# Output projections as sums of rounded products, and an experts' loop without its marker products

## Chip, cores and metric

The kernel runs on one core of a Trainium2 chip. The metric is the device time of one execution in microseconds: the median of the runs shown. TensorE (PE) does the matrix products, PEld its weight loads, VectorE (DVE) and ScalarE (ACT) the elementwise work, GpSimd (POOL) and SyncE (SP) start transfers; each engine works through its own instruction list in order, and semaphores tie the lists together.

## The reference

Two blocks work on 256 tokens of 1024 columns (the first also on 256 context tokens); all in float32.

```python
# first block, layer 0
y = concat([fourier_mix(a), neighborhood_attention(q, k, v, ...)]) @ w_out      # 512 tokens, 1024 x 1024
# both layers
for e in range(N_EXPERTS):                                                      # 16 experts, top 2 of them per token
    hid = silu(tok @ w1[e]) * (tok @ w3[e])
    out = out + gate[:, e:e + 1] * (hid @ w2[e])
# second block
y_a = (attention * silu(g_a)) @ w_proj_a                                        # 512 -> 1024
y_b = o_b @ w_proj_b                                                            # 1024 -> 1024
merged = sigmoid(zgate_a) * y_a + sigmoid(zgate_b) * y_b
h_res = h_res + merged @ w_out                                                  # 1024 -> 1024
```

## The kernel before

Activations lie transposed, 128 columns of the model on the partitions and the tokens along the free axis: `hT` is the residual stream, `XT` the working copy, `arena` a region that each stage lays out anew. All weights come through a ring of three slots of 2 MB (`ring`, `SLOTS`, `BLK`): SP waits until a slot is free (`w_free`), starts the load of the next block (L511), and readers wait for `w_full`. The order of the blocks is fixed (`B_MIX`, `B_MIXO`, `B_MOE0`, ...).

Most projections are already sums of rounded products. A weight part of 128 x 1024 elements is rounded by ACT to float32r (`..._hi`), DVE subtracts that from the weight and writes the rest back into the ring (`..._lo`), the activations are split in the same way, and TensorE adds three float32r products per step (`three_terms`, L622, and `quarter`, L721): high times high, low times high, high times low. Four places still use plain float32 products through `chain` (L576): the first block's output projection (L964 to L972, blocks `B_MIXO`, 8 tiles of 8 products with 512 tokens), the retention output projection (L1055), and in the second block `B_PA` (L1267, 8 tiles of 4 products with 256 tokens), `B_PB` (L1274, 8 tiles of 8) and `B_WO` (L1285, 8 tiles of 8). In the trace one float32 product in `chain` is two records.

The first of these follows the neighborhood attention loop (L923 to L962), which is a software pipeline over 24 pairs in `NA_PAIRS`: the first 12 have 512 keys, the last 12 have 256. In step i TensorE makes the scores of pair i (L930), turns the probabilities of pair i-2 (L945) and multiplies pair i-3 by the values (L959); DVE finds the row maximum (L1978), scales (L1984, L1986) and copies a result out (L1993); ACT copies (L1491) and exponentiates (L1499).

The experts' loop (`routed`) handles one expert per turn, and each layer has 16 turns. A turn has three blocks of four quarters: w1 (512 columns per product), w3 (256 columns) and w2 (512 columns), 24 products of `quarter` or `three_terms` for w1, 48 for w3, 24 for w2. `w_hi` and `w_lo` hold four quarters; ACT may round quarter q of the next block only when TensorE is done with quarter q of the present one, which it learns from `split_used`. [...] Where the last product of a quarter already raises another one (`f_u1`, `f_u3`, `f_d`), a marker product of two columns follows it and raises `split_used`:

```python
def used():
    nc.tensor.matmul(ps[0:32, 7, 0:2], tick[:, 0:32], tick[:, 0:2], start=True, stop=True).then_inc(split_used, 1)
```

That is four marker products (L588) in a turn: one behind w1, two in w3, one behind w2. `release` (L581) makes the same kind of product (L583) for the ring and stays.

The second block's attention (L1232 to L1263) is a similar pipeline over eight pairs in `AT_PAIRS`, with a DVE reduction (L2264), an ACT exponential (L1662), an ACT copy (L1657), turned probabilities (L1261) and the product with the values (L1252). Then come `B_PA`, `B_PB`, `B_WO` one after the other, each tile evicted by DVE (L2283; L2287 and L2288; L2291), and one transfer writes 1 MB to `out_d`.

## Time and profile before

| | us |
|---|---|
| time, median of 3 runs | 2014.21 (2013.33 to 2014.35) |
| the profiled execution's own time | 2023.89 |
| its span, first to last instruction | 2022.1 |
| TensorE busy in it | 1808.3 (89%) |
| VectorE / ScalarE busy | 1077.0 / 946.7 |
| mean granted TensorE clock | 0.942 of full speed |

The profile comes from one execution, so stages are compared inside it, and a difference in a stage is then set against the median. Busy TensorE time counts matmuls that overlap in the pipeline, so the distance between the starts of two matmuls says more than the duration of one.

### The profile page before, as it was taken

To read this page: it belongs to the slowest core of one execution; us is meant where nothing else is said; L and a number is where in the kernel's file an instruction comes from. 1 tells how busy PE (TensorE), PEld (TensorE's weight loads), DVE (VectorE), ACT (ScalarE), POOL (GpSimd) and SP (SyncE) were. 2 spreads that over 40 slices of the span, in tenths; PEclk is the share of its full clock that TensorE was granted. 3 is DMA by queue.
4 is the path that set the end of the run, shared out by engine and by line. 5 is a ranking of instruction groups with operands and counts; after the bars stand their busy time and mean duration, and the time that the engine had idled before them with its cause. 6 is when DMAs were issued, how large, how long until landed. Compare 5 with 4: busy or idle time off the path is not lost.

```text
span 2022.1 us, 27351 instructions
## 1 busy us (share of the span) xinstructions
PE 1808.3 (89%) x10936; PEld 1450.2 (72%) x10936; DVE 1077.0 (53%) x1423; ACT 946.7 (47%) x1234; POOL 60.9 (3%) x68
## 2 busy tenths in 40 slices
PE   5999998699999467999878789999947998999888
PEld 2786644588888437879757668888836988887677
DVE  3531623788888436243321278888835485534431
ACT  3323604588878315233320268788824472343320
POOL 0000000000000100000000010000000000100100
PEclk8999999799999778999989989999978999999899
DMA  8725014799999734224344369999951544263511
GB/s 333 149 108 208 1 42 173 284 379 389 384 377 380 293 122 160 84 88 162 126 166 167 146 262 385 371 392 383 368 223 67 187 167 149 69 203 145 146 43 63
DMA packets 52943, 421.68 MB, mean 209 GB/s; under 512 B 16996, under 2 KB 18148, under 8 KB 30576
## 3 DMA queue, kind: packets, MB, share of 16 engines
q1 hardware_dynamic: 26240, 364.55, 46.9%
q0 software_dynamic: 8592, 32.69, 5.2%
q10 hardware_dynamic: 18016, 23.07, 3.6%
q8 instruction: 73, 1.20, 0.2%
q14 instruction: 22, 0.18, 0.0%
HBM read 399.27 MB, written 21.02 MB: 208 GB/s over the span
## 4 chain that ended last, share of the span: by engine, by line
PE 84%; DVE 6%; DMA 3%; ACT 3%; issue 2%; POOL 0%; SPq 0%; DVEq 0%; ACTq 0%; POOLq 0%
PE ps L625 37%; PE ps L726 19%; PE ps L578 12%; PE ps L605 2%; PE ps L633 2%; PE ps L741 2%; PE ps L616 1%; PE ps L930 1%; PE ps L959 1%; PE ps L945 1%; DMA y_d<-arena 1%; PE ps L1120 1%; PE ps L748 1%; PE ps L588 1%; DMA hT<-h 1%
## 5 line engine op out<-in xcount | busy, mean ns | idle before, releaser
L1830 DVE TENSOR_TENSOR w_lo<-ring,w_hi 128x1024 fp32r<-128x1024 f32 x384 | 452.6, 1219 | 63.6 <-ACT w_hi L1366 63.6
L1366 ACT ACTIVATE w_hi<-ring 128x1024 fp32r<-128x1024 f32 x384 | 398.6, 1058 | 127.2 <-PE ps L588 43.2
L625 PE MATMUL ps<-XT_lo,arena_r 128*128 128x256 f32 (+1 forms) x1584 | 349.6, 297 | 8.9 <-DVE ring_r L2106 7.2
L625 PEld LDWEIGHTS ps<-XT_lo,arena_r 128*128 128x128 f32 x1584 | 260.9, 191 | 21.4 <-issue 7.9
L726 PE MATMUL ps<-w_hi,x_hi 128*128 128x256 f32 (+1 forms) x768 | 259.7, 338 | 4.8 <-issue 4.8
L726 PE MATMUL ps<-w_hi,x_lo 128*128 128x256 f32 (+1 forms) x768 | 246.3, 321 | 0.0
L726 PE MATMUL ps<-w_lo,x_hi 128*128 128x256 f32 (+1 forms) x768 | 246.2, 321 | 0.0
L625 PE MATMUL ps<-arena_r 128*128 128x512 f32 (+1 forms) x560 | 198.9, 355 | 15.6 <-DVE ring_r L2018 10.6
L2106 DVE TENSOR_TENSOR ring_r<-ring,arena_r 128x1024 fp32r<-128x1024 f32 x96 | 113.5, 1221 | 128.4 <-ACT arena_r L1588 128.3
L625 PE MATMUL ps<-XT_lo,ring_r 128*128 128x256 f32 x608 | 172.1, 283 | 0.0
L625 PE MATMUL ps<-w_hi,arena_r 128*128 128x512 f32 x512 | 161.1, 396 | 0.0
L726 PEld LDWEIGHTS ps<-w_hi,x_hi 128*128 128x128 f32 x768 | 146.5, 191 | 16.4 <-issue 5.6
L726 PEld LDWEIGHTS ps<-w_lo,x_hi 128*128 128x128 f32 x768 | 146.6, 191 | 11.2
L726 PEld LDWEIGHTS ps<-w_hi,x_lo 128*128 128x128 f32 x768 | 146.9, 191 | 9.7
L625 PEld LDWEIGHTS ps<-arena_r 128*128 128x128 f32 x560 | 107.5, 192 | 33.8 <-DVE ring_r L2018 10.7
L625 PE MATMUL ps<-arena_r,XT_lo 128*128 128x512 f32 (+1 forms) x352 | 126.1, 396 | 6.0 <-DVE XT_lo L2114 6.0
L578 PE MATMUL ps<-arena,ring 128*128 128x256 f32 x576 | 126.4, 381 | 1.3 <-DVE arena L2288 0.9
L625 PE MATMUL ps<-arena_r,ring_r 128*128 128x256 f32 (+1 forms) x368 | 125.2, 340 | 0.0
L2018 DVE TENSOR_TENSOR ring_r<-ring,arena_r 128x1024 fp32r<-128x1024 f32 x48 | 58.6, 1225 | 117.2 <-ACT arena_r L1526 117.1
L578 PEld LDWEIGHTS ps<-arena,ring 128*128 128x128 f32 x576 | 108.9, 190 | 16.0 <-DVE arena L2288 0.9
L625 PEld LDWEIGHTS ps<-XT_lo,ring_r 128*128 128x128 f32 x608 | 115.8, 190 | 0.0
L1306 ACT ACTIVATE XT<-hT 128x512 f32<-128x512 f32 (+1 forms) x48 | 20.5, 508 | 195.5 <-DVE hT L1881 66.7
(295 smaller groups left out, 2555.9 us busy)
## 6 DMA issues: line engine op xcount, KB each, us to landing
ring<-w_all SPq DMA_DIRECT2D x172, 2048.0 KB, 9.5
y_d<-arena ACTq DMA_DIRECT2D x32, 512.0 KB, 10.3
arena<-toep_d POOLq DMA_DIRECT2D x16, 384.0 KB, 8.7
arena<-rpb ACTq DMA_DIRECT2D x16, 192.0 KB, 5.9
xtok_d<-arena ACTq DMA_DIRECT2D x6, 512.0 KB, 2.7
hT<-h SPq DMA_DIRECT2D x1, 2048.0 KB, 13.2
arena<-cb_d POOLq DMA_DIRECT2D x1, 1536.0 KB, 7.3
out_d<-XT SPq DMA_DIRECT2D x1, 1024.0 KB, 4.8
```

What stands on the lines that cost most here:

```text
L578: last = nc.tensor.matmul(out, a, b, start=(i == 0), stop=(i == len(pairs) - 1))
L588: nc.tensor.matmul(ps[0:32, 7, 0:2], tick[:, 0:32], tick[:, 0:2], start=True, stop=True).then_inc(split_used, 1)
L605: last = nc.tensor.matmul(ps[32 * j:32 * j + 32, bank, :], c2s[:, 2 * k:2 * k + 32], w[:, k], start=(k < 4), stop=(k >= 4))
L625: last = nc.tensor.matmul(out, a, b, start=(first and i == 0), stop=(final and i == 2))
L633: last = nc.tensor.matmul(ps[:, 7, 0:b - a], ones, XT[:, k, a:b], start=(k == 0), stop=(k == KT - 1))
L726: last = nc.tensor.matmul(to, x[:, j, k], w[:, q, i * cols:(i + 1) * cols], start=(first and i == 0 and m == 0), stop=(final and i == len( ...
L741: last = nc.tensor.transpose(ps[:, k // 4, (k % 4) * P:(k % 4 + 1) * P], xg[:, j, k * P:(k + 1) * P], ident)
L1306: nc.scalar.activation(XT[:, k, a:b], hT[:, k, a:b], ACT.Square).then_inc(nm_sq, 1)
L1366: nc.scalar.activation(w_hi[:, q], slot(b, "p (q c) -> p q c", q=4)[:, q], ACT.Copy).then_inc(hi_rdy, 1)
L1830: nc.vector.tensor_tensor(w_lo[:, q], slot(base + n, "p (q c) -> p q c", q=4)[:, q], as_f32(w_hi[:, q]), ALU.subtract).then_inc(*split_sig ...
L2018: nc.vector.tensor_tensor(part_of(n, p % 4, p // 4 in RET_V, ring_r), part_of(n, p % 4, p // 4 in RET_V, ring), as_f32(ret_hi(p)), ALU.sub ...
L2106: nc.vector.tensor_tensor(z_part(p, ring_r), z_part(p, ring), as_f32(z_hi(p)), ALU.subtract).then_inc(dw_lo, 1)
```

## The change

- **Output projection of the first block.** The 8 tiles of `B_MIXO` become sums of three rounded products. ACT and DVE split the first five of its eight weight parts in steps 12 to 21 of the neighborhood attention loop (`mixo_split`) and the activations `XT` from step 13 on (`mixo_x`); the last three parts follow behind the loop.
- **Second block.** `B_PB` now lies ahead of `B_PA` in the ring. `B_PB`, `B_PA` and `B_WO` become sums of three rounded products, with 20 more weight parts (`last_split`), the splits of `g_b` (8), the attention output (4) and the merged gates (8). The first three tiles of `B_PB` (`gated_tile`) are put between the last steps of the attention loop.
- **Experts' loop.** `used()` is gone; ACT waits for `f_u1`, `f_u3` and `f_d` where those are raised, and for `split_used` elsewhere.
- **Output.** `out_d` is written in three transfers of 4, 3 and 1 of the 8 column groups, each as soon as they are there.
- The retention output projection stays in float32; its semaphores are only renamed.

```diff
@@ -68,9 +68,9 @@
 B_Z1 = B_IB + 2
 B_Z2 = B_Z1 + 12
 B_V2 = B_Z2 + 7
-B_PA = B_V2 + 3
-B_PB = B_PA + 1
-B_WO = B_PB + 2
+B_PB = B_V2 + 3
...
+        def mixo_free(p):
+            if p < 3:
+                return None
+            return (sx_s, len(NA_PAIRS) // 2) if p < 5 else (mx_mm, MIX_UNITS + p - 4)
...
+        def last_free(p):
+            n = len(AT_PAIRS)
+            if p < 2:
+                return z2_mm, 20
+            if p < 6:
+                return sx_neg, AT0 + n
+            if p < 12:
+                return yb_mm, p - 5
+            if p < 16:
+                return (sx_o, AT0 + n) if p == 15 else (sx_t, AT0 + n)
+            return ya_mm, 2 * (p - 15)
...
-            sp.wait_ge(yo_ev, KT)
-            sp.dma_start(out_d, XT[:, :, LAT]).then_inc(out_done, 16)
-            sp.wait_ge(out_done, 16)
+            for a, b in ((0, 4), (4, 7), (7, KT)):
+                sp.wait_ge(yo_ev, b)
+                sp.dma_start(out_d[:, a:b], XT[:, a:b, LAT]).then_inc(out_done, 16)
+            sp.wait_ge(out_done, 48)
...
-            def used():
-                nc.tensor.matmul(ps[0:32, 7, 0:2], tick[:, 0:32], tick[:, 0:2], start=True, stop=True).then_inc(split_used, 1)
...
-                    if done is None:
-                        last.then_inc(split_used, 1)
-                    else:
-                        last.then_inc(done, 1)
-                        used()
...
                         if k < 3:
                             last.then_inc(split_used, 1)
-                    used()
...
-                              (split_used, 192)):
+                              (split_used, 128)):
...
-            pe.sem_inc(split_used, 4)
+            pe.sem_inc(split_used, 3)
...
-            pe.wait_ge(sx_ev, len(NA_PAIRS))
             for b in range(2):
-                arrive(B_MIXO + b)
-                w = slot(B_MIXO + b, "p (k m) -> p k m", k=KT)
                 for m in range(4):
                     u = 4 * b + m
                     if u >= 4:
                         pe.wait_ge(mx_ev, MIX_UNITS + u - 3)
-                    chain(ps[:, u % 4, :], [(w[:, k, m * P:(m + 1) * P], XT[:, k]) for k in range(KT)]).then_inc(mx_mm, 1)
+                    pe.wait_ge(dw_lo, DW_MO + u + 1)
+                    w, w2 = mo_w[u % 5], part_of(B_MIXO + b, m, False, ring_r)
+                    for k in range(KT):
+                        if u == 0:
+                            pe.wait_ge(nm_lo, LO_MO + k + 1)
+                        last = three_terms(ps[:, u % 4, :], w[:, k], w2[:, k], mo_x[:, k], XT_lo[:, k], k == 0, k == KT - 1)
+                    last.then_inc(mx_mm, 1)
+                if b == 0:
+                    pe.wait_ge(sx_ev, len(NA_PAIRS))
                 release(B_MIXO + b)
             norm(1)
...
+            def last_tile(p, out, x_hi, x_lo, first_x=None, tile=slice(0, P)):
+                w, w2 = last_hi(p), last_part(p, ring_r)
+                pe.wait_ge(dw_lo, DW_LAST + p + 1)
+                n = 4 if 8 <= p < 12 else KT
+                for k in range(n):
+                    if first_x is not None:
+                        pe.wait_ge(nm_lo, first_x + k + 1)
+                    last = three_terms(out, w[:, k, tile], w2[:, k, tile], x_hi[:, k], x_lo[:, k], k == 0, k == n - 1)
+                return last
+            def gated_tile(m):
+                if m >= 4:
+                    pe.wait_ge(yb_ev, m - 3)
+                if m == 0:
+                    pe.wait_ge(sx_neg, AT0 + len(AT_PAIRS))
+                last_tile(m, ps[:, m % 4, 0:SEQ], g_hi, g_lo, LO_G if m == 0 else None).then_inc(yb_mm, 1)
+                if m % 4 == 3:
+                    release(B_PB + m // 4)
...
+                if i >= len(AT_PAIRS):
+                    gated_tile(i - len(AT_PAIRS))
...
+            for m in range(3, 8):
+                gated_tile(m)
+            pe.wait_ge(sx_c, AT0 + len(AT_PAIRS))
             for m in range(8):
-                if m >= 4:
-                    pe.wait_ge(ya_ev, m - 3)
-                chain(ps[:, m % 4, 0:SEQ], [(w[:, k, m * P:(m + 1) * P], z2[:, k]) for k in range(4)]).then_inc(ya_mm, 1)
+                if m >= 3:
+                    pe.wait_ge(ya_ev, m - 2)
+                last_tile(8 + m // 2, ps[:, 4 + m % 3, 0:SEQ], at_hi, at_lo, LO_AT if m == 0 else None,
+                          slice(m % 2 * P, m % 2 * P + P)).then_inc(ya_mm, 1)
             release(B_PA)
...
-            pe.wait_ge(yb_ev, KT)
-            for m in range(8):
-                if m % 4 == 0:
-                    arrive(B_WO + m // 4)
-                    w = slot(B_WO + m // 4, "p (k m) -> p k m", k=KT)
-                if m >= 4:
-                    pe.wait_ge(yo_ev, m - 3)
-                chain(ps[:, m % 4, 0:SEQ],
-                      [(w[:, k, (m % 4) * P:(m % 4 + 1) * P], zgA[:, k]) for k in range(KT)]).then_inc(yo_mm, 1)
+                pe.wait_ge(*((yo_ev, m - 3) if m >= 4 else (yb_ev, KT)))
+                last_tile(12 + m, ps[:, m % 4, 0:SEQ], zg_hi, zg_lo, LO_ZG if m == 0 else None).then_inc(yo_mm, 1)
...
-                        act.wait_ge(split_used, e * 12 + (q0 + 4 * n + q + 1))
+                        if (n, q) == (1, 3):
+                            act.wait_ge(f_u1, e + (c + 1))
+                        elif n == 2 and q % 2:
+                            act.wait_ge(f_u3, e * 2 + (2 * c + 1 + q // 2))
+                        elif q < 3:
+                            act.wait_ge(split_used, e * 8 + (8 * c + (1, 4, 7)[n] + (q // 2 if n == 2 else q)))
+                        elif layer or not isinstance(e, int) or e:
+                            act.wait_ge(f_d, e * 2 + 2 * c)
...
+            def mixo_split(p):
+                n = B_MIXO + p // 4
+                if p % 4 == 0:
+                    act.wait_ge(w_full[n % SLOTS], 16 * (n // SLOTS + 1))
+                if mixo_free(p):
+                    act.wait_ge(*mixo_free(p))
+                nc.scalar.activation(mo_w[p % 5], part_of(n, p % 4, False, ring), ACT.Copy).then_inc(dw_hi, 1)
+            def mixo_x(k):
+                if k < 2:
+                    act.wait_ge(fn_ev, 8)
+                    act.wait_ge(sx_s, len(NA_PAIRS) // 2)
+                else:
+                    act.wait_ge(sx_ev, len(NA_PAIRS) // 2 + 2 * (k - 1))
+                nc.scalar.activation(mo_x[:, k], XT[:, k], ACT.Copy).then_inc(xo_hi, 1)
...
+                if i in (12, 14, 16, 18, 20):
+                    mixo_split(i // 2 - 6)
+                if i in (13, 15):
+                    mixo_x((i - 13) // 2)
+                if i >= 17 and i % 2:
+                    mixo_x((i - 13) // 2)
+            mixo_x(7)
+            for p in range(5, 8):
+                mixo_split(p)
...
+                if 4 <= u < 12:
+                    act.wait_ge(hg_done, HG // 2)
+                    nc.scalar.activation(g_hi[:, u - 4], g_b[:, u - 4], ACT.Copy).then_inc(xo_hi, 1)
...
+            def last_split(p):
+                n = B_PB + p // 4 if p < 8 else B_PA if p < 12 else B_WO + (p - 12) // 4
+                if p % 4 == 0:
+                    act.wait_ge(w_full[n % SLOTS], 16 * (n // SLOTS + 1))
+                act.wait_ge(*last_free(p))
+                nc.scalar.activation(last_hi(p), last_part(p, ring), ACT.Copy).then_inc(dw_hi, 1)
+            def attended_hi(hp):
+                act.wait_ge(sx_ev, AT0 + 2 * hp + 2)
+                nc.scalar.activation(at_hi[:, hp], z2[:, hp], ACT.Copy).then_inc(xo_hi, 1)
+            last_split(0)
+            last_split(1)
...
+                if i in (5, 7, 9):
+                    attended_hi((i - 5) // 2)
+                if i >= len(AT_PAIRS):
+                    last_split(i - len(AT_PAIRS) + 2)
...
+            last_split(4)
+            last_split(5)
+            attended_hi(3)
+            for p in range(6, 16):
+                last_split(p)
+            for m in range(8):
+                act.wait_ge(yb_ev, KT + m + 1)
+                nc.scalar.activation(zg_hi[:, m], zgA[:, m], ACT.Copy).then_inc(xo_hi, 1)
+                if m % 2:
+                    last_split(16 + m // 2)
...
+                if i in (13, 15, 17, 19, 21):
+                    mixo_split((i - 13) // 2)
+                if i in (14, 16) or i >= 18 and i % 2 == 0:
+                    mixo_x((i - 14) // 2)
+            mixo_x(7)
             for m in range(8):
+                if m < 3:
+                    mixo_split(5 + m)
...
+                if 69 < p < 86 and p % 2 == 0:
+                    k = (p - 70) // 2
+                    dve.wait_ge(xo_hi, KT + k + 1)
+                    nc.vector.tensor_tensor(g_lo[:, k], g_b[:, k], as_f32(g_hi[:, k]), ALU.subtract).then_inc(nm_lo, 1)
...
+            def last_split(p):
+                dve.wait_ge(dw_hi, DW_LAST + p + 1)
+                nc.vector.tensor_tensor(last_part(p, ring_r), last_part(p, ring), as_f32(last_hi(p)), ALU.subtract).then_inc(dw_lo, 1)
+            def attended_lo(hp):
+                dve.wait_ge(xo_hi, 2 * KT + hp + 1)
+                nc.vector.tensor_tensor(at_lo[:, hp], z2[:, hp], as_f32(at_hi[:, hp]), ALU.subtract).then_inc(nm_lo, 1)
+            def gated_out(m):
+                dve.wait_ge(yb_mm, m + 1)
+                nc.vector.tensor_tensor(zgB[:, m], zgB[:, m], ps[:, m % 4, 0:SEQ], ALU.mult).then_inc(yb_ev, 1)
+            last_split(0)
+            last_split(1)
             for i in range(len(AT_PAIRS) + 3):
                 if i < len(AT_PAIRS):
...
+                if i in (6, 8, 10):
+                    attended_lo((i - 6) // 2)
+                if 8 <= i < 10:
+                    last_split(i - 6)
+            last_split(4)
+            last_split(5)
+            attended_lo(3)
+            for m in range(8):
+                gated_out(m)
+                if m < 6:
+                    last_split(6 + m)
+            for p in range(12, 16):
+                last_split(p)
+            def summed_lo(m):
+                dve.wait_ge(xo_hi, 2 * KT + 4 + m + 1)
+                nc.vector.tensor_tensor(zg_lo[:, m], zgA[:, m], as_f32(zg_hi[:, m]), ALU.subtract).then_inc(nm_lo, 1)
             for m in range(8):
                 dve.wait_ge(ya_mm, m + 1)
-                nc.vector.tensor_tensor(zgA[:, m], zgA[:, m], ps[:, m % 4, 0:SEQ], ALU.mult).then_inc(ya_ev, 1)
...
+                nc.vector.tensor_tensor(zgA[:, m], zgA[:, m], ps[:, 4 + m % 3, 0:SEQ], ALU.mult).then_inc(ya_ev, 1)
+                if m:
+                    summed_lo(m - 1)
+                dve.wait_ge(ya_ev, m + 1)
                 nc.vector.tensor_tensor(zgA[:, m], zgA[:, m], zgB[:, m], ALU.add).then_inc(yb_ev, 1)
+                if m % 2 and m > 1:
+                    last_split(16 + m // 2 - 1)
+            summed_lo(KT - 1)
+            last_split(19)
```

## Rows read from the trace of the kernel before

**Rows 1.** The page: busy times, and the chain that ended last, by line.
```profile
PE 1808.3 (89%) x10936; PEld 1450.2 (72%) x10936; DVE 1077.0 (53%) x1423; ACT 946.7 (47%) x1234; POOL 60.9 (3%) x68
PE ps L625 37%; PE ps L726 19%; PE ps L578 12%; PE ps L605 2%; PE ps L633 2%; PE ps L741 2%; PE ps L616 1%; PE ps L930 1%; PE ps L959 1%; PE ps L945 1%; DMA y_d<-arena 1%; PE ps L1120 1%; PE ps L748 1%; PE ps L588 1%; DMA hT<-h 1%
```

**Rows 2.** The chain that ended last, two turns' first products: start, us.
```profile
395.00 5.69 PE ps L726 x24
...
414.17 5.69 PE ps L726 x24
```

**Rows 3.** The timeline of TensorE around one marker product.
```profile
380.92 0.39 PE L726 MATMUL ps<-w_hi,x_lo 128*128 128x512 f32 x1
381.15 0.39 PE L726 MATMUL ps<-w_lo,x_hi 128*128 128x512 f32 x1
381.47 0.18 PE L588 MATMUL ps<-tick 128*32 128x2 bf16 x1
381.57 0.38 PE L726 MATMUL ps<-w_hi,x_hi 128*128 128x256 f32 x1
381.80 0.28 PE L726 MATMUL ps<-w_hi,x_lo 128*128 128x256 f32 x1
381.91 0.28 PE L726 MATMUL ps<-w_lo,x_hi 128*128 128x256 f32 x1
```

**Rows 4.** Busy time by stretch: one turn, then two stretches of the start.
```profile
core 0: us, PE busy (x) PEld busy (x) DVE busy (x) ACT busy (x) POOL busy (x), PEclk, DMA share, GB/s
419.15:438.30 19.15, 19.15 (x114) 16.33 (x113) 16.51 (x19) 15.46 (x18) 1.05 (x1) 1.00 0.97 382
6.00:12.00 6.00, 2.69 (x16) 0.60 (x16) 0.17 (x1) 0.00 (x0) 0.00 (x0) 1.00 1.00 425
```

**Rows 5.** The loop's VectorE timeline: four subtractions of w3.
```profile
417.93 4.63 DVE L1830 TENSOR_TENSOR w_lo<-ring,w_hi 128x1024 fp32r<-128x1024 f32 x4 [1.41 <-ACT w_hi L1366]
```

**Rows 6.** The chain again: float32 tiles and three-product tiles.
```profile
74.63 22.39 PE ps L625 x96
...
260.36 27.73 PE ps L578 x64
288.20 27.68 PE ps L578 x64
...
1761.41 11.50 PE ps L625 x96
...
1973.55 14.03 PE ps L578 x64
1988.53 27.91 PE ps L578 x128
```

**Rows 7.** Busy time of the neighborhood attention's second half, columns as in rows 4.
```profile
232.00:260.40 28.40, 27.29 (x263) 17.96 (x257) 21.91 (x69) 21.75 (x67) 0.00 (x0) 1.00 0.01 2
```

**Rows 8.** Groups of split instructions: name, count, busy, mean ns, idle before.
```profile
L1440 ACT ACTIVATE arena_r<-ring 128x1024 fp32r<-128x1024 f32 x20 | 20.8, 1053 | 2.3 <-DMA ring<-w_all 2.3
L1957 DVE TENSOR_TENSOR XT_lo<-XT,arena_r 128x512 fp32r<-128x512 f32 x8 | 5.5, 693 | 0.3
L2283 DVE TENSOR_TENSOR arena<-arena,ps 128x256 f32<-128x256 f32 x8 | 3.4, 421 | 11.2 <-PE ps L578 11.2
L1499 ACT ACTIVATE arena<-ps,arena 128x256 f32<-128x256 f32 (+1 forms) x26 | 12.4, 488 | 0.0
```

**Rows 9.** Chain and timeline at the second attention's start and end.
```profile
1895.44 0.96 DVE L2264 CUSTOM_DVE_ANT_0 arena<-ps,arena 128x768 f32<-128x768 f32 x1 [8.09 <-PE ps L1239]
...
1937.28 1.46 ACT arena L1657
1938.79 1.53 PE ps L1252 x24
1940.32 1.48 PE ps L1261 x12
1943.32 1.55 PE ps L1252 x24
```

**Rows 10.** Transfers: KB each, us from issue to landing.
```profile
out_d<-XT SPq DMA_DIRECT2D x1, 1024.0 KB, 4.8
sm<-smalls SPq DMA_DIRECT2D x1, 187.5 KB, 2.4
toep_d<-arena POOLq DMA_DIRECT2D x1, 48.0 KB, 3.8
```

**Rows 11.** Two stretches with a lower granted clock, columns as in rows 4.
```profile
751.00:756.00 5.00, 4.29 (x20) 1.32 (x20) 0.00 (x0) 0.59 (x1) 0.00 (x0) 0.50 0.91 390
1537.00:1551.00 14.00, 13.84 (x48) 10.77 (x48) 12.67 (x23) 9.81 (x12) 0.00 (x0) 0.80 0.00 0
```

More of the change, by code:

```diff
@@ L70 @@
 B_V2 = B_Z2 + 7
-B_PA = B_V2 + 3
-B_PB = B_PA + 1
-B_WO = B_PB + 2
+B_PB = B_V2 + 3
+B_PA = B_PB + 2
+B_WO = B_PA + 1
 N_BLK = B_WO + 2
@@ L203, in build @@
         with nc.sbuf_tensor("arena_r", [P, 30400], F32R) as arena_r:
+            pass
+        with nc.sbuf_tensor("below_lo", [P, 6144], F32), nc.sbuf_tensor("last_lo", [P, 4096], F32R) as last_lo:
             pass
@@ L422, in mix_free, with last_hi, last_part @@
             return mx_mm, {19: 18}.get(p, p - 4)
+        mo_x = area_r(7168, 4096).rearrange("p (k t) -> p k t", k=KT)
+        mo_w = [area_r(at, 1024).rearrange("p (k m) -> p k m", k=KT) for at in (13312, 14336, 15360, 11264, 12288)]
+        def mixo_free(p):
+            if p < 3:
+                return None
+            return (sx_s, len(NA_PAIRS) // 2) if p < 5 else (mx_mm, MIX_UNITS + p - 4)
+        g_hi, g_lo = hT_r[:, :, CTX], last_lo[:, 0:2048].rearrange("p (k t) -> p k t", k=KT)
+        at_hi, at_lo = XT_lo[:, 0:4, CTX], XT_lo[:, 4:KT, CTX]
+        zg_hi, zg_lo = hT_r[:, :, CTX], last_lo[:, 2048:4096].rearrange("p (k t) -> p k t", k=KT)
+        def last_hi(p):
+            if p < 8 and p % 6 < 2:
+                return XT_lo[:, :, SEQ + p % 6 * P:SEQ + p % 6 * P + P]
+            at = 1024 * (p % 4 - 2) if p in (2, 3) else 1024 * (p - 2) if p < 6 else 1024 * (p % 4)
+            if 12 <= p < 16:
+                at = (12288, 26112, 27648, 4608)[p - 12]
+            return area_r(at, 1024).rearrange("p (k m) -> p k m", k=4 if 8 <= p < 12 else KT)
+        def last_part(p, of):
+            if p < 8:
+                return part_of(B_PB + p // 4, p % 4, False, of)
+            if p >= 12:
+                return part_of(B_WO + (p - 12) // 4, p % 4, False, of)
+            s = of[:, (B_PA % SLOTS) * BLK:(B_PA % SLOTS + 1) * BLK].rearrange("p (k m) -> p k m", k=4)
+            return s[:, :, (p - 8) * SEQ:(p - 7) * SEQ]
+        def last_free(p):
[9 more added lines that the diff above has]
+            return ya_mm, 2 * (p - 15)
         RET_V = range(4, 8)
@@ L727, in quarter @@
                                                     start=(first and i == 0 and m == 0), stop=(final and i == len(ks) - 1 and m == 2))
[L728 to L732 removed]
+                    last.then_inc(split_used if done is None else done, 1)
                 def turn_rows(e, j, half_e, first):
@@ L1060, in _ @@
                     if u >= 4:
-                        pe.wait_ge(y_ev, u - 3)
-                    chain(ps[:, u % 4, 0:SEQ], [(w[:, k, m * P:(m + 1) * P], gR[:, k]) for k in range(16)]).then_inc(y_mm, 1)
+                        pe.wait_ge(rp_ev, 48 + u - 3)
+                    chain(ps[:, u % 4, 0:SEQ], [(w[:, k, m * P:(m + 1) * P], gR[:, k]) for k in range(16)]).then_inc(rp_mm, 1)
                 release(B_RETO + b)
```

44 lines of the change are left out of this document (20 added, 24 removed).

## The prediction

> **What bounds the kernel now.** I read the page first: TensorE is busy 89% of the span, and the chain that ended last is matmuls for the most part, with L625 (three-product tiles and w2), L726 (w1 and w3) and L578 (float32 chains) at 37, 19 and 12% [rows 1]. So what counts is how densely TensorE's list is packed, stage by stage. Then the chain in order of time gave the length of a turn of the experts' loop: the same product comes back after 414.17 - 395.00 = 19.17 us, and 32 turns are 613 us [rows 2]. The busy times by stretch show that in a turn TensorE is busy for all 19.15 us, VectorE 16.51, ScalarE 15.46, and the DMA engines at a share of 0.97 [rows 4]. TensorE sets the pace, but three others are close behind, DMA closest. The timeline of TensorE shows what a marker product costs, the chain once more what a float32 tile and a three-product tile take, and the stretches of both attention loops how much room ACT and DVE have there.
>
> **The change, part by part: the marker products.** Products of w1 start 0.23 us apart, those of w3 0.12. Around a marker, the last w1 product starts at 381.15 and the second w3 product at 381.80: 0.65 us, where 0.23 + 0.12 = 0.35 would do [rows 3]. The marker costs 0.30 us, more than its own slot, since the pipeline of weight loads behind it starts anew. Four in a turn, 128 in all: 128 x 0.30 = 38.4 us, all of it on TensorE, which has no gap there. A turn would be 19.15 - 1.20 = 17.95 us. ACT's waits come no later than before, since they now hang on the last product itself.
>
> What could take some of it: VectorE's 16.51 us and ScalarE's 15.46 fit into 17.95. The quarters are in time too: DVE subtracts those of w3 from 417.93 on, four in 4.63 us, so the first is there at about 419.1, and TensorE comes to w3 at about 420.0 [rows 2, 5]; that margin of 0.9 shrinks by the 0.3 of the marker behind w1 and the 0.1 by which ACT's copy is tied to the end of w2. DMA is the open term. A turn moves 382 GB/s x 19.15 us = 7.3 MB at a share of 0.97. If its packets keep their present cost, the floor is 0.97 x 19.15 = 18.6 us; if they get as cheap as in the saturated start, where a share of 1.00 moved 425 GB/s, it is 7.3 / 0.425 = 17.2 us [rows 4]. The second is nearer to what a fuller queue looks like, but a turn also has 4 KB packets. I take 1.10 us a turn instead of 1.20: 32 x 1.10 = 35.2 us; ends 32 x 0.55 = 17.6 and 38.4.
>
> The Trainium skill has a rule that speaks against this part: "DMA: Bandwidth & Descriptors", section "Where 436 GB/s comes from", holds that for transfers between HBM and SBUF a limit of about 358 GB/s per core binds, and 435 GB/s is the ceiling of the fabric. By the first, 7.3 MB would need 20.4 us, and the removal would bring nothing at all; by the second, 16.8 us, and it would bring everything. The stretches above disagree with the first figure (382 and 425 GB/s) and fit the second.
>
> **The first block's output projection.** Eight float32 tiles take 27.73 + 27.68 = 55.4 us; four three-product tiles with 512 tokens take 22.39, so eight take 44.9 with the seams [rows 6]. That is 10.5 us less, and the first tile no longer waits for the last copy-out, 0.3 more. The price is in the attention loop ahead. Its second half lasts 28.1 us with TensorE at 27.3; DVE is busy 21.9 and ACT 21.8 [rows 7]. Into it go, on DVE, five weight parts of 1.2 us and seven of the eight activation splits of 0.69: 10.9 us; on ACT five of 1.05 and as many copies of about 0.6: 9.5 [rows 5, 8]. DVE then needs 32.8 us for a stretch of 28.1, at least 4.7 longer. By its order it is more: one pair of steps has 2 x 1.6 us of its own work and 1.85 of splits, 5.1 us where TensorE needs 3.6; over ten steps that is 7.5, and about 1.5 of it fits into the gaps of steps 13 to 15, where TensorE's steps are still long. I take 6.0 (ends 4.7 and 9). Net: 10.8 - 6.0 = 4.8 us. The last three weight parts lie behind 5.6 us tiles; nothing there.
>
> **The second block's tail.** From 1937.26, where TensorE has nothing to do but wait for a copy of ACT, to 2016.44 are 79.2 us before. With TensorE never waiting it would be 8 tiles of `B_PB` and 8 of `B_WO` at 11.50 / 4 = 2.88 each, 8 of `B_PA` at half, the three pieces of attention 1.53 + 1.48 + 1.55, and 0.3 for seams: 62.4 us, 16.8 less [rows 6, 9]. A quarter of that is the waits of 1.5 us for ACT's copies, now filled by the first tiles. Against it:
> - Two weight parts on DVE stand ahead of the first reduction, which begins at 1895.44 and is on the chain [rows 9]. ACT finishes the first of them near 1894.8, DVE both near 1897.1: 1.6 us.
> - Two of the four `attended_hi` (0.45 each) stand ahead of copies that TensorE waits for: 0.9.
> - DVE's list behind `B_PB`. Its last `gated_out` ends 0.4 us after the eighth tile, TensorE then does `B_PA` in 11.5 us and wants the first gates. DVE has four weight parts (4.7), then for each of eight m a product, a subtraction that waits for ACT's rounding of the sum before, and a sum, 0.42 + 0.15 + 0.42 + 0.42 = 1.4 with `zg_hi` at 0.49, three more weight parts (3.5), and the last subtraction (1.0): 20.5 us to the end [rows 8]. TensorE waits until 0.4 + 20.5, less 11.5 and the 2.5 of the tile that it does meanwhile: 6.9, I take 6.6 (ends 3 and 10). The three weight parts of `B_WO` inside the loop are what is late.
>
> So 16.8 - 1.6 - 0.9 - 6.6 = 7.7 us. The splits of `g_b` lie beside the z products, where both engines are idle more than half of the time, and cost nothing. The last transfer is 128 KB instead of 1 MB: 4.8 us becomes something between the 2.4 of 187.5 KB and the 3.8 of 48 KB, I take 3.1: 1.7 us [rows 10]. Tail: 9.4 us.
>
> **Sum.** 35.2 + 4.8 + 9.4 = 49.4 us. The profiled execution took 2023.9 us, so its like becomes 1974.5; the median of the runs lies 9.7 below it, so 2014.2 - 49.4 = 1964.8, and I say 1965.
>
> **Rivals.**
> - *DMA becomes the bound of the experts' loop* (0.22). For it: a share of 0.97. Against it: 425 GB/s at a share of 1.00, and ACT waits for no load in the loop now. At 18.6 us a turn the loop gives 17.6: 2014.2 - 17.6 - 14.2 = 1982.
> - *The splits eat the projections' gain* (0.11). DVE is the bound in both places; if each split in the attention loop stalls the chain by its full length (10.9 instead of 6.0) and the tail waits 10 instead of 6.6, and TensorE comes out of those waits at half clock for some 3 us, the projections give about 3: 2014.2 - 35.2 - 3 = 1976.
> - *The markers were not on the path* (0.03). If TensorE only trades them for waits on quarters, the loop stays at 19.15: 2014.2 - 14.2 = 2000. Against it: TensorE's list has no gap.
> - *Slower: a stall in every turn that costs the clock* (0.04). If a late load or quarter lets TensorE stand in each turn, its granted clock may fall, as it did to 0.50, the level of 1.2 GHz, in the stretch at 751, and stay at 0.80 on average for 14 us behind a wait at 1537 [rows 11]. At half clock the 48 products of w3 would take 5.7 us more. If only half of that and a 1.2 us stall come in, a turn is 17.95 + 2.9 + 1.2 = 22.0 us, and the kernel 2014.2 + 32 x 2.9 - 14.2 = 2093. It ends slower from 19.15 + 14.2 / 32 = 19.6 us a turn on. Against it: 1.00 in the whole loop, with margins that stay above zero. The Trainium skill ("TensorE: Matmul & The Clock Gate", Part 1) says that the clock is halved by idleness and released by activity; the rows agree.
>
> **Range and chances.** The forecast has 0.60, between 2014.2 - 38.4 - 22 = 1954 (TensorE never waits in the loop, and half of the tail's wait is gone) and 1974. The first rival and most of the second are taken in up to 1984. Range 1954 to 1984. A measurement of this kernel tells 0.2% (4 us) from no change. Faster 0.94, within 0.2% 0.02, slower 0.04.
>
> **What would show it.** Turns of 18.0 to 18.1 us, with no L588 group left; a DMA share of 0.99 or more, and no wait of ACT for a load. If turns are near 18.6 and ACT waits for DMA, the first rival holds. The second half of the neighborhood attention lasts about 34 us with DVE above 90% busy, eight tiles of 5.6 us behind it. In the tail, TensorE works between the attention's last copies, waits about 6 us in the first tile of `B_WO` for the subtractions of the gates, and the last matmul to the end of the span takes 4 us instead of 5.6. The prediction is wrong if loads arrive late in the loop, or if DVE's walk through its list is not as I laid it out.

## The result, and the profile after

The changed kernel takes 1967.68 us (median of 4 runs, 1965.79 to 1968.80), the kernel before 2014.28 beside it (4 runs, 2013.33 to 2019.15): the ratio is 0.9763, 95% interval 0.9745 to 0.978, and 46.6 us are gone. The forecast was 1965, in a range of 1954 to 1984. The profiled execution took 1968.8 us with a span of 1966.8.

The page of the kernel after, its busy lines and the chain that ended last, against [rows 1]:

```profile
PE 1750.6 (89%) x11032; PEld 1448.5 (74%) x11032; DVE 1113.8 (57%) x1479; ACT 979.6 (50%) x1290; POOL 68.6 (3%) x68
...
PE 81%; DVE 9%; DMA 4%; ACT 4%; issue 2%; POOL 0%; SPq 0%; ACTq 0%; DVEq 0%; POOLq 0%
```

TensorE is 57.7 us less busy and still sets nearly everything. To see where the time went, I cut the chain of four profiled executions at the same landmarks (all numbers are starts of rows of the chain or differences of them; norm 1 and norm 2 are the normalizations ahead of and behind the first experts' loop, "markers out alone" and "both new orders" are experiments described below):

| stage, from | before | after | markers out alone | after, both new orders |
|---|---|---|---|---|
| 1 start to norm 1 (holds the first block's output projection) | 317.49 | 311.68 | 318.41 | 306.02 |
| 2 norm 1 to the first w1 product | 55.85 | 57.51 | 56.08 | 56.79 |
| 3 experts' loop 0 | 309.61 | 293.48 | 293.32 | 292.41 |
| 4 write of `y_d` to norm 2 | 52.16 | 45.92 | 47.80 | 46.94 |
| 5 norm 2 to loop 1 | 439.70 | 439.04 | 437.45 | 440.64 |
| 6 experts' loop 1 | 309.95 | 292.83 | 292.97 | 292.75 |
| 7 to the last group of z products | 401.79 | 401.68 | 401.08 | 401.75 |
| 8 tail | 135.55 | 124.66 | 134.29 | 118.40 |
| span | 2022.10 | 1966.80 | 1981.40 | 1955.70 |

The two loops give 33.3 us, stage 1 gives 5.8, the tail 10.9. Stage 4 gives 6.2, and that is no work of the change: the run with the markers out alone has 47.8 there, the run with the projections alone, markers kept, 47.0. The profiled execution before had 5 us more in it; it also lay 9.7 us above its median. In its chain TensorE stands for 4.13 us at 725.29, a gap for which the profile names no releaser, and none of the 13 other traces has it. Stage 2 looks 1.7 us worse, but over all profiled executions with the new first projection it lies between 55.3 and 57.6.

One turn of the loop in the chain of after, against [rows 2]:

```profile
385.21 5.48 PE ps L671 x24
390.69 9.75 PE ps L772 x60
400.44 0.22 PE ps L790 x2
400.66 1.44 PE ps L772 x12
402.10 0.87 PE ps L783 x8
402.97 0.22 PE ps L790 x2
403.19 5.49 PE ps L671 x24
```

From one group of w2 products to the next are 403.19 - 385.21 = 17.98 us, and no marker lies in between. Over the next 14 turns it is (643.71 - 390.69) / 14 = 18.07 us. Busy times by stretch (length; busy us and instructions of PE, PEld, DVE, ACT, POOL; granted clock, DMA share, GB/s) of one turn and of those 14, against [rows 4]:

```profile
400.00:418.10 18.10, 18.10 (x111) 16.18 (x110) 16.23 (x18) 14.75 (x18) 1.29 (x1) 1.00 0.99 409
390.69:643.71 253.02, 252.97 (x1513) 224.50 (x1513) 229.48 (x240) 213.56 (x238) 15.80 (x12) 1.00 0.99 402
```

The granted clock is 1.00, the level of 2.4 GHz; DMA moves 402 GB/s at a share of 0.99. What was waited for from 390 to 650 (in total, times, longest):

```profile
...
ACT w_hi L1427 <- ACT arena L1451: 5.5, 9, 0.7
PEld ps L772 <- DVE w_lo L1950: 2.2, 5, 0.5
ACT w_hi L1427 <- DMA ring<-w_all: 1.7, 3, 0.9
```

TensorE now and then waits for a quarter. ACT waits for a load three times, 1.7 us in all, where the prediction named "no wait of ACT for a load" as a sign; what that costs, the run with less DMA below tells. The second half of the neighborhood attention, against [rows 7], and the projection behind it in the chain, against [rows 6]:

```profile
232.00:265.16 33.16, 27.90 (x263) 18.06 (x259) 30.05 (x79) 29.64 (x79) 0.00 (x0) 1.00 0.00 1
```

```profile
PEld ps L986 <- DVE arena L2118: 9.5, 12, 1.2
```

```profile
265.16 22.39 PE ps L671 x96
287.66 22.41 PE ps L671 x96
...
311.68 7.13 PE ps L679 x16
```

DVE is busy 91% of the half, ACT 89%, TensorE 84%. What TensorE's weight loads wait for is DVE's scaling (L2118), and from 237.72 to 260.98 the chain is DVE's list alone: DVE is busy 22.9 of these 23.3 us, ACT 21.1. The eight tiles take 5.6 us each. The tail's chain, against [rows 6, 9]:

```profile
1911.16 11.54 PE ps L671 x96
...
1922.84 8.89 DMA ring<-w_all
...
1931.75 1.06 ACT arena_r L1749
1932.81 0.32 ACT hT_r L1785
...
1940.67 1.14 DVE ring_r L2403
1941.81 0.34 DVE last_lo L2459
...
1942.20 21.93 PE ps L671 x171
...
1964.15 0.42 DVE XT L2474
```

At 1922.8 TensorE gives the last slot of `B_PB` back, the load of `B_WO`'s second block takes 8.89 us, ACT stands on it with the first weight part of that block (L1749), and the copies of the gated sums (L1785) queue behind. Then DVE's list, weight parts (L2403) among them, leads to the last projection. TensorE comes out of these waits at a lower clock: for 3 us from 1942.20 on the granted clock is 0.50, the level of 1.2 GHz, and then 1.00 again:

```profile
1942.20:1945.20 3.00, 3.00 (x14) 3.00 (x15) 1.47 (x2) 0.00 (x0) 0.00 (x0) 0.50 0.00 0
```

The last copy-out ends at 1964.57, the span at 1966.8: 2.2 us, before 5.2.

### The profile page after: what moved, and what is told of

Read it like the earlier page. It is cut to its first block, busy times and chain, and to the rows that moved or that the text cites. A ratio compares the mean times of both kernels' runs of the same rounds, so it can differ in the third digit from the quotient of the medians.

```text
span 1966.8 us, 27611 instructions
## 1 busy us (share of the span) xinstructions
PE 1750.6 (89%) x11032; PEld 1448.5 (74%) x11032; DVE 1113.8 (57%) x1479; ACT 979.6 (50%) x1290; POOL 68.6 (3%) x68
## 4 chain that ended last, share of the span: by engine, by line
PE 81%; DVE 9%; DMA 4%; ACT 4%; issue 2%; POOL 0%; SPq 0%; ACTq 0%; DVEq 0%; POOLq 0%
PE ps L671 42%; PE ps L772 18%; PE ps L628 6%; PE ps L651 2%; PE ps L679 2%; PE ps L783 1%; PE ps L662 1%; DMA ring<-w_all 1%; DMA y_d<-arena 1%; DMA xtok_d<-arena 1%; PE ps L1166 1%; PE ps L790 1%; PE ps L971 1%; DMA hT<-h 1%; PE ps L1239 1%
## 5 line engine op out<-in xcount | busy, mean ns | idle before, releaser
L671 PE MATMUL ps<-XT_lo,arena_r 128*128 128x256 f32 (+1 forms) x1712 | 386.6, 300 | 11.2 <-DVE ring_r L2245 7.2
L671 PEld LDWEIGHTS ps<-XT_lo,arena_r 128*128 128x128 f32 x1712 | 283.7, 190 | 27.0 <-issue 7.9
L772 PE MATMUL ps<-w_hi,x_hi 128*128 128x256 f32 (+1 forms) x768 | 250.8, 327 | 4.9 <-issue 4.8
L671 PE MATMUL ps<-arena_r 128*128 128x512 f32 (+1 forms) x624 | 224.2, 359 | 15.6 <-DVE ring_r L2157 10.6
L671 PE MATMUL ps<-XT_lo,ring_r 128*128 128x256 f32 x640 | 182.0, 284 | 0.0
L772 PEld LDWEIGHTS ps<-w_lo,x_hi 128*128 128x128 f32 x768 | 147.4, 192 | 10.5
L671 PE MATMUL ps<-arena_r,ring_r 128*128 128x512 f32 (+1 forms) x432 | 150.4, 348 | 0.0
L671 PEld LDWEIGHTS ps<-arena_r 128*128 128x128 f32 x624 | 119.4, 191 | 36.9 <-DVE ring_r L2157 10.6
L671 PEld LDWEIGHTS ps<-XT_lo,ring_r 128*128 128x128 f32 x640 | 121.9, 190 | 0.0
L1676 ACT ACTIVATE arena_r<-ring 128x1024 fp32r<-128x1024 f32 x96 | 96.6, 1053 | 21.6 <-PE ps L671 20.1
L671 PEld LDWEIGHTS ps<-w_hi,arena_r 128*128 128x128 f32 x512 | 93.8, 188 | 17.9
L1361 ACT ACTIVATE XT<-hT 128x512 f32<-128x512 f32 (+1 forms) x48 | 20.5, 508 | 165.6 <-DVE hT L2001 67.1
```

The costliest lines, as they stand in the source:

```text
L671: last = nc.tensor.matmul(out, a, b, start=(first and i == 0), stop=(final and i == 2))
L772: last = nc.tensor.matmul(to, x[:, j, k], w[:, q, i * cols:(i + 1) * cols], start=(first and i == 0 and m == 0), stop=(final and i == len( ...
L1361: nc.scalar.activation(XT[:, k, a:b], hT[:, k, a:b], ACT.Square).then_inc(nm_sq, 1)
L1676: nc.scalar.activation(z_hi(p), z_part(p, ring), ACT.Copy).then_inc(dw_hi, 1)
```

## The experiments

Kernels of one group ran on one chip, and the kernel before beside each group (medians 2019.75, 2019.56 and 2020.89, 9 runs each, with a spread of up to 11 us of its own). The record names chip 15 for the first two groups, chip 1 for the third, and none for the result above. Ratios are to the kernel before, with 95% intervals; small differences I take between kernels of one group and from the stages of the traces. The changed kernel itself ran only for the result (1967.68) and in the third group (1966.78), so a difference of the first two groups to it crosses groups and is less certain by some us.

**First group: the parts.**

*Markers out alone*, on the kernel before:

```diff
-                    if done is None:
-                        last.then_inc(split_used, 1)
-                    else:
-                        last.then_inc(done, 1)
-                        used()
+                    last.then_inc(split_used if done is None else done, 1)
```

> The kernel before with the marker products alone taken out of the experts' loop; all projections as before. If a marker costs TensorE 0.27 to 0.30 us wherever it stands, and nothing takes its place, the loops shrink as they do in the full change: 32 turns by 1.07 less about 1 for the first turns, 33 us, so about 1981 us, turns of 18.0 to 18.1. If the loop's gain in the full change owed something to the other edits (buffers that come free earlier, other clocks), it is below 30 us here (over 1984).

1983.32 us, ratio 0.9822 (0.9803 to 0.9841). Loops of 293.3 and 293.0 us, the same as in the full change, 33.3 us below before: the loop's gain is the markers' alone. The median is 2 us above the 1981 expected.

*Markers out and the first projection new*, the tail as before:

> Markers out and the first block's output projection as three products; the second block's tail as before. If the projection's 5.8 us reach the end, about 4 to 6 us below the run with the markers alone, 1976 us. If they are lost again in the routing phase behind it, where the full change needs 57.5 us instead of 55.9, within 2 us of that run, or about 4 if only that 1.65 is lost. The rest to 1967.7, then 8 to 9 us, would be the tail's.

1978.03 us, ratio 0.9793 (0.9776 to 0.9811): 5.3 us below the run with the markers alone; to the changed kernel's 1967.7 are then 10.3 for the tail. The projection's gain reaches the end, and is not lost in the routing behind it.

*Projections alone*, markers put back into the changed kernel:

> The changed kernel with the marker products and ACT's waits on them put back. If the parts add up, 1967.7 + 33 = 2001 us, turns of 19.13 us again. If the two parts get in each other's way (the projections' splits and the loop's copies share ACT and DVE only in different phases, so I don't expect it), the sum of this run's gain and that of the markers alone differs from 46.6 us by more than 3.

1998.41 us, ratio 0.9891 (0.9874 to 0.9909). Against the changed kernel, putting the markers back costs 30.7 us by the medians and 31.1 by the spans, and putting the projections back (the first run) 15.6 and 14.6: together 46.3, so the parts add up. Counted against the kernel before in this group, the two gains are 36.4 + 21.3 = 57.8 instead, 11 more than the 46.6 of the result, and by the letter of what I wrote that says that they don't. But the full change's own gain moves as well: in the third group it is 2020.89 - 1966.78 = 54.1, with the changed kernel as fast as before and the kernel before 6.6 us slower. Against that the two gains are 3.7 too many. So the parts add up to within some 4 us, and no closer; why the kernel before is 5 to 7 us slower in the groups is open.

One turn in this kernel's chain shows what each marker (L638) costs:

```profile
404.07 5.48 PE ps L675 x24
409.54 0.11 PE ps L638
409.65 5.69 PE ps L776 x24
415.33 0.11 PE ps L638
415.44 3.06 PE ps L776 x24
418.50 0.11 PE ps L638
418.61 1.62 PE ps L776 x12
...
420.45 1.43 PE ps L776 x12
421.87 0.11 PE ps L638
421.98 1.02 PE ps L791 x8
```

Behind w2, behind w1 and inside w3 a marker takes 0.1 and makes the group behind it 0.2 longer (the last 12 products of w3 take 1.43, the 12 behind a marker 1.62). Ahead of the turned rows (L791) it makes 1.02 out of 0.87: 0.10 + 0.15. The w2 products of the next turn start at 423.22, so the turn is 423.22 - 404.07 = 19.15 us.

*Less DMA*, the changed kernel with half of each w2 block left out (`short` is the slot of w2 inside the experts' loops):

```diff
+                        if j == short:
+                            to, of = to[:, 0:2048], of[:, 0:2048]
                         sp.dma_start(to, of).then_inc(w_full[j], 16)
```

> The changed kernel, but of every w2 block of the experts only the first half is loaded (1 MB less of 7.3 MB a turn; the other half holds whatever was in the buffer, so the output isn't the reference's). All instructions on the engines stay. If the loop is TensorE's alone, turns go from 18.05 to no less than 18.0 and the kernel stays within 2 us of 1967.7. If the DMA engines, at a share of 0.99, already set part of the pace (late quarters now and then, a gather that lands in 10.7 us), the stalls of some tenths of a us go, turns are 17.95 and the kernel is 3 to 4 us faster. Below 17.9 a turn, the price of TensorE's own products would hang on DMA traffic, which neither theory says.

1963.32 us, ratio 0.9721 (0.9701 to 0.9742). The same 14 turns and the same waits as above:

```profile
387.49:640.34 252.85, 252.79 (x1514) 224.52 (x1513) 229.49 (x240) 213.96 (x238) 15.60 (x12) 1.00 0.92 345
```

```profile
PEld ps L783 <- DVE w_lo L1961: 2.2, 5, 0.5
```

The share falls from 0.99 to 0.92, ACT waits for no load any more, and the turn stays at 18.06 us; TensorE's 2.2 us of waits for quarters are still there, so they are no matter of DMA either. The loop is not bound by DMA. The whole kernel is 4.4 us below 1967.68 all the same (3.5 below the 1966.78 of the third group), which by its size alone is the "3 to 4 us faster" of the other theory. In the profiled execution, 7.3 us shorter, 2.2 of it lie in stage 2 and 4.0 between loop 1 and the end of stage 7, 3.6 of them behind that loop, and the turns have next to none of it. Two profiled executions of the unedited changed kernel differ by 5.9 (1966.8 and 1960.9), so I read nothing into it.

**Second group: what a marker costs, and two new orders.**

*Two spare markers* at each of the four places of the changed kernel:

```diff
+            def spare():
+                nc.tensor.matmul(ps[0:32, 7, 0:2], tick[:, 0:32], tick[:, 0:2], start=True, stop=True)
+                nc.tensor.matmul(ps[0:32, 7, 0:2], tick[:, 0:32], tick[:, 0:2], start=True, stop=True)
```

> The changed kernel with two marker products in a row, that signal nothing, at each of the four places of a turn where the kernel before had one. If each marker costs its own 0.27 to 0.30 us, a turn is 18.05 + 8 x 0.28 = 20.3 us and the kernel about 2040 us. If the cost is mostly what the first one does to the full-size products around it (the pipeline of weight loads starts anew), the second costs no more than its slot, about 0.05 to 0.1 us: a turn is 18.05 + 4 x 0.28 + 4 x 0.07 = 19.4 us, the kernel about 2012. If the price hung on the semaphores that the markers carried, and not on the products, it is below 19.0.

2000.68 us, ratio 0.9917 (0.9889 to 0.9944). A turn is 419.24 - 400.00 = 19.24 us, one marker at each place makes 19.15: the second one costs 0.02 us a place, less than either forecast. The price is paid once a place, and not for the semaphore, since these markers carry none.

*A marker of the same type*, one at each place:

```diff
+                def spare(j):
+                    nc.tensor.matmul(ps[0:32, 7, 0:2], x_hi[:, j, 0, 0:32], x_hi[:, j, 0, 0:2], start=True, stop=True)
```

> The changed kernel with one product of the markers' size (32 columns of weights, 2 of data) at each of the four places, but in the rounded fp32 type of the products around it instead of bf16, and with no semaphore. If the small size costs, it is as dear as the old marker, 0.27 us: turns of 19.1 us, 2001 us. If the change of type and back costs, it is nearly free: turns of 18.05 + 4 x 0.07 = 18.3 us or less, about 1976 us.

1977.35 us, ratio 0.9789 (0.9765 to 0.9814). A turn is 18.36 us, 0.09 more a place than the 17.98 without. TensorE's timeline behind w1, here and with the two bf16 markers (start, length, tile, type):

```profile
395.41 0.39 PE L772 MATMUL ps<-w_lo,x_hi 128*128 128x512 f32 x1
395.64 0.17 PE L780 MATMUL ps<-x_hi 128*32 128x2 f32 x1
395.67 0.36 PE L772 MATMUL ps<-w_hi,x_hi 128*128 128x256 f32 x1
395.87 0.28 PE L772 MATMUL ps<-w_hi,x_lo 128*128 128x256 f32 x1
```

```profile
394.66 0.39 PE L777 MATMUL ps<-w_lo,x_hi 128*128 128x512 f32 x1
394.98 0.18 PE L638 MATMUL ps<-tick 128*32 128x2 bf16 x1
395.02 0.16 PE L639 MATMUL ps<-tick 128*32 128x2 bf16 x1
395.11 0.39 PE L777 MATMUL ps<-w_hi,x_hi 128*128 128x256 f32 x1
```

From the last w1 product to the second w3 product are 0.46 us with the marker of the same type, 0.65 with one bf16 marker [rows 3], 0.35 with none. Two thirds of the price is the other type. Going to bf16 costs 0.09 (the marker starts 0.32 behind the last w1 product instead of 0.23), coming back 0.10. The weight loads, in the same two runs, show what goes with it:

```profile
395.42 0.11 PEld L780 LDWEIGHTS ps<-x_hi 128*32 128x32 f32 x1
```

```profile
394.98 0.09 PEld L638 LDWEIGHTS ps<-tick 128*32 128x32 bf16 x1 [0.35 <-issue]
```

The load for the marker of the same type starts 0.22 us ahead of its product, under the last w1 product; the bf16 one stands idle for 0.35 and starts together with its product. The two markers also read different tiles (`x_hi`, `tick`); in the last group a marker that still reads `tick`, but in the rounded type, saves as much (0.57 instead of 0.76 us), so which tile is read isn't the cause.

*Weight parts later*: seven of the first projection's eight behind the attention loop, on ACT and DVE alike:

```diff
-                if i in (12, 14, 16, 18, 20):
+                if i in (12, 14, 16, 18, 20)[:1]:
                     mixo_split(i // 2 - 6)
```

> The changed kernel, but only the first weight part of the first block's output projection is rounded and subtracted inside the attention loop; the other seven behind it, beside the projection's own tiles of 5.6 us. If DVE's list sets the second half of the loop, four parts less are 4 x 1.15 = 4.6 us less of 33.2 (no less than TensorE's own 27.9), and norm 1 begins near 307 instead of 311.7: about 4.5 us faster than the changed kernel, ratio to the kernel before 0.974. If the loop hangs on ACT or on the order of the activation splits instead, the half stays above 31 us; if the second tile waits for its part, 1 to 2 us come back there.

1965.58 us, ratio 0.9732 (0.9711 to 0.9753). The projection starts at 259.85 instead of 265.16, and norm 1 at 306.37, 5.3 us earlier, where 4.5 were expected; of these 5.3 the medians show 2.1 (to 1967.68) or 1.2 (to 1966.78):

```profile
232.00:259.85 27.85, 26.64 (x255) 17.66 (x253) 24.74 (x72) 24.96 (x74) 0.00 (x0) 1.00 0.00 1
```

The half is TensorE's again, and the later tiles wait for nothing. The edit takes the four parts off ACT's list as well as DVE's; that DVE's was the bound rests on the chain and the waits above.

*Another order in the tail*:

```diff
-                if m % 2:
-                    last_split(16 + m // 2)
+            for p in range(16, 20):
+                last_split(p)
...
-            for p in range(12, 16):
-                last_split(p)
+            last_split(12)
...
-                if m % 2 and m > 1:
-                    last_split(16 + m // 2 - 1)
...
+            last_split(13)
+            last_split(14)
             for m in range(8):
+                if m < 5:
+                    last_split(15 + m)
                 dve.wait_ge(yo_mm, m + 1)
```

> The changed kernel with another order in the tail: behind the last gate DVE takes one weight part instead of four, the loop over the gated sums has no weight parts in it on either engine, and the other seven come behind it, in between the copy-outs of the last projection. If DVE's list and ACT's wait for the late load are what TensorE waits for (7.1 us between 1922.7 and 1964.1 beyond eight tiles of 1.43 and eight of 2.84), all but about 1 us of it goes: 6 us faster than the changed kernel, ratio 0.973, first tile of the last projection complete near 1937. If the loop's own round trips between DVE and ACT (1.25 us for each of eight) set its length whatever stands in it, the gain is 3 us or less.

1962.47 us, ratio 0.9719 (0.9698 to 0.9741). Its tail takes 118.3 us instead of 124.7:

```profile
1919.42 11.52 PE ps L671 x96
...
1932.97 1.14 DVE ring_r L2403
...
1934.25 20.16 PE ps L671 x168
...
1954.43 0.42 DVE XT L2474
```

From the start of `B_PA` to the last copy-out are 35.0 us, where TensorE's products alone need 3 x 11.52 = 34.6. In the changed kernel it was 41.3. The 6.3 are more than waits: the last 168 products start 0.120 us apart at a granted clock of 1.00, where the last 171 of the changed kernel take 21.93 us, 0.128 each.

**Third group: what adds up.**

*The changed kernel again*:

> The changed kernel once more, unedited, beside the three runs that follow, for their comparison: ratio 0.976 within 0.003, turns of 18.05 us.

1966.78 us, ratio 0.9735 (0.972 to 0.975). Its own time is that of the result above within 1 us; the ratio moved with the kernel before.

*Both new orders*:

> The changed kernel with both new orders: seven of the eight weight parts of the first block's output projection behind the attention loop, and the tail's weight parts in between the last copy-outs. They lie 1600 us apart and share nothing, so their gains add: 5.3 us (the projection's start at 259.85 instead of 265.16) and 6.3 us (118.3 instead of 124.7 us from the last z product group to the end), 11.6 us below the unedited changed kernel on the same chip. If a gain early in the kernel is lost in the transfers of the routing phases, it is nearer to 7.

1956.76 us, ratio 0.9683 (0.967 to 0.9696): 10.0 us below the unedited changed kernel by the medians, 11.9 by stages 1 and 8 of the table (12.6 against the changed kernel of the same group). At their places the gains add; the 1.6 us short of 11.6 in the medians are within what stages 4 and 5 differ among executions.

*The other 50 markers in the rounded type*, on top of that:

```diff
-        tick = ctx.enter_context(nc.sbuf_tensor("tick", [P, 32], mybir.dt.bfloat16))
+        tick = ctx.enter_context(nc.sbuf_tensor("tick", [P, 32], F32R))
```

> As the kernel with both new orders, and the 50 marker products that are left outside the experts' loops (they give buffers back) take the rounded fp32 type instead of bf16. If the change of type costs 0.2 us wherever a marker stands between rounded products, and some 35 of the 50 do on TensorE's own path, it is 5 to 7 us faster than that kernel. If most of them stand next to waits, or next to four-pass fp32 products that are a change of type anyway, it is within 2 us.

1950.31 us, ratio 0.9654 (0.9641 to 0.9667), 6.5 us less again, the fastest kernel here. But the chain shows two effects. Here, and in the kernel with both orders:

```profile
74.03 21.88 PE ps L671 x96
```

```profile
73.46 22.39 PE ps L671 x96
```

Around a marker 0.57 us pass instead of 0.76 (95.52 to 96.09, 95.46 to 96.22), which over 50 markers is at most 9.5 us. And elsewhere products with 512 tokens start 0.228 us apart instead of 0.233 where no marker is near, while groups of 96 with 256 tokens take 11.61 instead of 11.51. The edit also makes the tile 128 bytes a partition instead of 64, so that every tile placed after it lies elsewhere; whether that or the type sets these distances isn't told apart. But in the changed kernel, too, 24 products of w2 take 5.48 us, 0.228 each, and 96 of the first projection 22.39, 0.233 each, all with a bf16 `tick`, so such a difference needs no change of type. The 6.5 us are what was forecast; that the markers alone earn them is not shown.

*One last transfer*, the changed kernel with `out_d` written at once:

> The changed kernel with the output written in one transfer of 1 MB behind the last copy-out, as before the change. From the end of the last copy-out to the end of the span: 2.2 us with three transfers, 5.2 in the kernel before. If the size of the last transfer is what the split saves, 5.2 again and 3.0 us slower than the unedited changed kernel; the 1.7 us of my prediction would be 3.9.

1970.49 us, ratio 0.9751 (0.9737 to 0.9765), 3.7 us above the unedited one, where 3.0 were expected. From the end of the last copy-out (1963.48) to the end of the span (1968.7) are 5.2 us, as before. Issue to landing by size, in the changed kernel:

```profile
out_d<-XT SPq DMA_DIRECT2D x1, 512.0 KB, 2.9
...
out_d<-XT SPq DMA_DIRECT2D x1, 128.0 KB, 1.8
```

## Why the prediction was right, step by step

- **Markers (35.2 predicted, 33.3 measured in the stages).** The turn of 18.05 us was forecast to 0.02, partly for a wrong reason. I took 0.10 off for DMA; taking 1 MB of DMA out of a turn gives nothing back, so that term is zero. What takes its place: the fourth marker, ahead of the turned rows in plain float32, costs 0.25, not 0.30; 3 x 0.30 + 0.25 = 1.15, which leaves 18.00, and a turn without waits is 17.98. TensorE waits for a quarter 5 times in 14 turns; on the chain that is 253.02 - 14 x 17.98 = 1.3 us, and makes the turn 18.07 on average. That is the margin of 0.9 us that I saw shrink; I took it to hold in every turn. And 32 turns was too many: the first of layer 0 lasts 16.02 us from the first w1 product to w2 (369.19 to 385.21), before 16.08, so it gains nothing.
- **The reason for 0.30 us** ("the pipeline of weight loads behind it starts anew") was too coarse. The load behind the marker does start with its product and not ahead of it, but it does so behind a marker of the same type too, which costs 0.09. The rest comes with the change of type.
- **First projection (4.8 predicted, 5.8 measured; 5.3 by the run without the tail).** Tiles: from their start to norm 1 57.13 us before, 46.52 after, 10.6 less as forecast (10.5). The attention half grew by 4.8 instead of 6.0, with DVE as its bound; moving four parts out took it all back. Most of the difference: instructions that follow each other on DVE without a wait take 1.13 and 0.60 us for the two kinds of splits instead of the 1.2 and 0.69 that I took, so a pair of steps is 4.77 us (242.79 to 247.56) instead of 5.1.
- **Tail (9.4 predicted, 10.9 measured).** Ahead of the first reduction 1.5 us were lost (from z's end, 1848.66 to 1852.54, 3.9; before 2.4), predicted 1.6. The two `attended_hi` on the chain take 0.30 and 0.31 instead of 0.45 each. From `B_PA` on TensorE loses 41.3 - 34.6 = 6.7 us, predicted 6.6, and that agreement is luck. TensorE waits for 5.3 us, and the other 1.4 are products behind the waits at the lower clock (21.93 us for 171 instead of 20.5), which I had only in a rival. DVE's walk from the last gate (1923.16) to the last subtraction (1942.15) takes 19.0 us instead of 20.5. Of these, 1.8 are a wait behind a late load that I had not foreseen, since I never asked when the block's slot comes free; so the walk itself is 17.2, 3.3 shorter than reckoned, as short instructions in a row follow each other in 0.33 us and I took 0.42. The waits don't lie where I put them either: 2.7 us stand in `B_PA`, which takes 14.2 us instead of 11.5 because the gates, whose products free the banks of `ps` for its next tiles, stand behind four weight parts in DVE's list, and 2.5 in the first tile of `B_WO`, where I had said about 6. The last transfer gave 3.0 instead of 1.7: I had bounded 128 KB by 2.4 and 3.8 us, it lands in 1.8.
- **Rivals.** DMA as the bound of the loop fell twice: turns of 18.07 instead of 18.6, and the run with less DMA. By the Trainium skill's figure of 358 GB/s ("DMA: Bandwidth & Descriptors", section "Where 436 GB/s comes from") a turn would be over 20 us; 402 GB/s over 14 turns disagree, and stay below the 435 of the same section. The splits did not eat the projections' gain (it is 15 to 17 us, by the first run and by stages 1 and 8), the markers were on the path, and TensorE's granted clock stayed at 1.00 in the turns, so nothing came of the slower case. What the second rival said of the clock, half of it for some 3 us behind the waits, did happen in the tail, for 1.4 us.
- **The sum** (49.4) is 2.8 above the 46.6 measured. The stages that the change touches give 33.3 + 5.8 + 10.9 = 50.0; the rest of the gap to the medians is within what executions of the kernel before differ among themselves. In the third group the same two kernels differ by 54.1, above the forecast, so no agreement closer than some 4 us counts for anything. The three parts were off by -1.9, +1.0 and +1.5, and that these nearly cancel is luck as well; that each part came out on its own, with the path and the bound that I had named, is not.

## What to carry to other kernels

A product that only raises a semaphore cost 0.09 us here where it had the type of its neighbours, and 0.25 to 0.30 where TensorE changed type for it; best is to let waiters hang on a product that signals anyway. When an engine's list becomes the bound of a stage through splitting work, look for the stage just behind it whose tiles are long: seven parts of 1.2 us vanished beside tiles of 5.6, and as many beside the last copy-outs, for 10 us together. Count what a wait costs behind it too: 5.3 us of waits in the tail brought 1.4 us of slower products. A share of 0.99 of the DMA engines did not mean that the loop waited for them: ask who does.

## What was unexpected

- A second bf16 marker behind the first costs 0.02 us, one of the neighbours' type 0.09, a first one of bf16 0.25 to 0.30.
- With the DMA engines at a share of 0.99, cutting 14% of the bytes (share 0.92) moved the turn by 0.01 us.
- Doubling a tile of 64 bytes a partition, with its type, went with a distance of 0.228 instead of 0.233 us between products of 512 columns, and with 0.1209 instead of 0.1199 between those of 256.
